# Where a large tile's step turns the next head's q and k: ahead of the second map's scores, or behind them

## The reference

```python
q, k, v = jnp.split(h @ w_in, 3, axis=-1)
q = rms_norm(q.reshape(B, S, H, 2, Dh), q_g)      # H = 8, Dh = 64, two maps per head
k = rms_norm(k.reshape(B, S, H, 2, Dh), k_g)
# per block of 128 queries, chunk-causal mask, scale Dh ** -0.5
s = jnp.where(mask, jnp.einsum('bqhmd,bshmd->bhmqs', qi, k) * scale, -jnp.inf)
p = jax.nn.softmax(s, axis=-1)
pd = p[:, :, 0] - lam * p[:, :, 1]
o = jnp.einsum('bhqs,bshe->bqhe', pd, v)
```

## Time and profile before

| | |
|---|---|
| median of three runs | 2813.56 us (2813.12 to 2814.98) |
| the profiled execution | 2813.21 us, its span 2811.4 us, granted clock 0.992 |
| busy of the span | PE 2725.0 us, PE's weight loads 2373.5, DVE 1898.9, ACT 1501.2, POOL 1077.1 |
| instructions | 42849 |
| longest groups of the attention on PE | projection L417 589.9 and 344.9 us, values L662 279.6 and L664 243.3, scores L559 255.8 and L561 232.5, turned probabilities L634 175.3, turned q and k L509 76.8 |

### The profile page before, as it was taken

One profiled execution on the slowest core, in us unless ns is written; L12 is line 12 of the kernel. 1 busy time (PEld: TensorE's weight loads), 2 busy tenths in 40 slices (PEclk: granted clock), 3 DMA queues, 4 the chain that ended last, 5 costly groups with the idle time before them and its releaser, 6 DMA issues.

```text
span 2811.4 us, 42849 instructions
## 1 busy us (share of the span) xinstructions
PE 2725.0 (97%) x14784; PEld 2373.5 (84%) x14784; DVE 1898.9 (68%) x2726; ACT 1501.2 (53%) x2987; POOL 1077.1 (38%) x956
## 2 busy tenths in 40 slices
PE   7999999999999999979999989999999999999999
PEld 7998989989898999967887778888888888888887
DVE  6777787777778787775776666555555555666655
ACT  5666666666666666654454434444444444344443
POOL 5633334243333424331000444444443444444443
PEclk9999999999999999989999999999999999999999
DMA  8742424243242423224455986666667976666663
GB/s 267 265 138 91 156 96 160 92 145 112 97 150 96 150 96 133 92 90 144 168 173 193 357 330 239 236 236 266 265 242 283 350 286 234 232 235 238 237 237 131
DMA packets 181808, 544.09 MB, mean 194 GB/s; under 512 B 14736, under 2 KB 88208, under 8 KB 136592
## 3 DMA queue, kind: packets, MB, share of 16 engines
q1 hardware_dynamic: 180016, 541.25, 52.8%
q10 hardware_dynamic: 1632, 0.79, 0.1%
HBM read 470.81 MB, written 71.17 MB: 193 GB/s over the span
## 4 chain that ended last, share of the span: by engine, by line
PE 81%; issue 7%; DVE 5%; ACT 3%; DMA 3%; POOL 1%; SPq 1%; ACTq 0%; POOLq 0%; DVEq 0%
PE banks L2159 21%; PE banks L2135 21%; PE banks L417 17%; PE banks L662 5%; PE banks L559 4%; PE banks L561 4%; PE banks L634 3%; PE banks L821 2%; PE banks L664 2%; PE banks L509 2%; DVE mx L578 1%; ACT p_all L601 1%; ACT pt_hi L643 1%; DVE p_all L623 1%; DMA u_factors<-y_stage 1%
## 5 line engine op out<-in xcount | busy, mean ns | idle before, releaser
L2135 PE MATMUL banks<-u,w 128*128 128x512 f32 x2688 | 614.6, 390 | 3.0 <-issue 2.3
L417 PE MATMUL banks<-w_hi,u_ring 128*128 128x384 f32 x2048 | 589.9, 348 | 10.9 <-DVE u_ring L1311 4.3
L2135 PEld LDWEIGHTS banks<-u,w 128*128 128x128 f32 x2688 | 505.4, 188 | 109.2 <-issue 3.3
L2159 PE MATMUL banks<-w,a_hi 128*128 128x512 f32 x1792 | 553.6, 390 | 7.1 <-DVE y L2057 7.1
L1900 POOL TENSOR_TENSOR w<-w_raw,w 128x1024 fp32r<-128x1024 f32 x96 | 246.2, 2578 | 559.5 <-DVE a_lo L2038 281.6
L601 ACT ACTIVATE p_all<-banks,bias 128x1024 f32<-128x1024 f32 (+7 forms) x384 | 331.6, 866 | 182.7 <-DVE bias L581 116.2
L2159 PEld LDWEIGHTS banks<-w,a_hi 128*128 128x128 f32 x1792 | 337.4, 188 | 77.6 <-issue 7.4
L417 PEld LDWEIGHTS banks<-w_hi,u_ring 128*128 128x128 f32 x2048 | 376.4, 189 | 15.6 <-issue 9.7
L2159 PE MATMUL banks<-w,a_lo 128*128 128x512 f32 x896 | 349.4, 390 | 0.0
L447 POOL TENSOR_TENSOR qk_rs<-qk_var,minus_half 128x4 f32<-128x4 f32 x128 | 129.4, 1011 | 564.3 <-DVE qk_var L441 564.3
L417 PE MATMUL banks<-w_lo,u_ring 128*128 128x384 f32 x1024 | 344.9, 337 | 0.0
(11 more groups left out here) (151 smaller groups left out, 4730.5 us busy)
## 6 DMA issues: line engine op xcount, KB each, us to landing
u<-u_factors SPq DMA_DIRECT2D x224, 1024.0 KB, 9.5
u_ring<-u_scratch SPq DMA_DIRECT2D x112, 1024.0 KB, 5.2
w_raw<-in_mlp_w SPq DMA_DIRECT2D x128, 512.0 KB, 6.7
u_scratch<-u_ring SPq DMA_DIRECT2D x16, 1024.0 KB, 5.0
u_factors<-q_hi SPq DMA_DIRECT2D x23, 512.0 KB, 4.4
u_factors<-q_lo SPq DMA_DIRECT2D x23, 512.0 KB, 4.5
w_raw<-in_a_w_in SPq DMA_DIRECT2D x90, 128.0 KB, 4.6
p_all<-in_x SPq DMA_DIRECT2D x16, 512.0 KB, 5.9
```

The lines of the kernel that those rows point to most:

```text
L417: last = pe.matmul(proj[:, 0:3 * HD], u[:, part, kt, :], w[:, kt, :], start=(kt == 0 and part == 0 and w is w_hi), stop=(kt == KT - 1 and ...
L2135: last = pe.matmul(banks[:, UP_BANKS[p] + f, :], w[:, 2 * k2 + k, f * P:(f + 1) * P], u[:, :, part, k, :], start=(STARTS[p] and k2 == 0 an ...
L2159: last = pe.matmul(banks[:, DOWN_BANKS[p] + t, :], a[:, p % 2, f, t * P:(t + 1) * P], b[:, f, :], start=(STARTS[p] and f == 0 and a is a_h ...
```

## The change

In `big_step` of TensorE the four transposes of q and k move from behind the projection's first half to behind the second map's scores, directly ahead of the first turned block of probabilities. In `big_step` of ScalarE the two copies move from behind the first map's exponentials to directly ahead of the copy of that first block. VectorE's and GpSimd's order, `turn_order` with its banks, and all waits stay.

```diff
@@ scalar, big_step
             for k in range(np):
                 act_exp(act, a, 0, k)
-            if n - 1 < ALL:
-                act_turned_qk(act, n - 1)
             if j > BIG:
                 act_square_output(act, a - 2)
             if t >= 1:
                 act_turned_u2(act, t - 1)
             if j == NT - 1 and h + 2 < H:
                 act_split_weights(act, h + 2, (0, 1))
+            if n - 1 < ALL:
+                act_turned_qk(act, n - 1)
             act_turned_p(act, a - 1, 0)
@@ tensor, big_step
             if n < ALL:
                 pe_project(pe, n, 0)
-            if n - 1 < ALL:
-                pe_turn_qk(pe, n - 1)
             if t >= 0:
                 pe_product(pe, t, 0)
                 pe_turn_u2(pe, t - 1)
             pe_scores(pe, a, 1)
+            if n - 1 < ALL:
+                pe_turn_qk(pe, n - 1)
             if t >= 0:
                 pe_product(pe, t, 1, (0,))
             pe_turn_p(pe, a - 1, 0)
```

## The result

| | before | after |
|---|---|---|
| median of 4 runs each | 2814.02 us | 2858.9 us |
| lowest to highest | 2813.12 to 2814.98 | 2857.33 to 2861.84 |
| span of the profiled execution | 2811.4 us | 2855.5 us |
| ratio after / before as recorded | | 1.0152, 95% interval 1.014 to 1.0165 (the two medians alone: 1.0159) |

The account below looks back on a forecast made before the run. TensorE, matmuls filling 97% of the span, was taken to bound the kernel. Later second turned blocks (39.6 us) plus what is late next (2.8) gave 42.4 on 2813.2: 2856 us, own range 2846 to 2866 (0.75), wider range 2837 to 2870.

Parts of the forecast that it names:

- Where: Steps with tiles 8 to 15 in heads 0 to 6, 56 in all, get longer; small steps and MLP as before.
- The scores don't come sooner: Second map's scores: still wait for the first map's exponentials in tiles 8 and 12 to 15; 0.43 us sooner in tile 9.
- The chain X + 2.41: X is the end of the second map's scores; the second L634 can't start before 2.41 us after it.
- The shifts of the second L634: Second block of turned probabilities, tiles 8 to 15: starts 0.49 to 0.93 us later, 5.66 a head, 39.6 in seven.
- What the wait would look like: Idle time on L634 put down to L536 in about 56 steps, 0.4 to 0.5 us each.
- What is late next: Behind L536 in VectorE's queue: the wide maximum and its exponential delay the next scores, 0.4 us a head, 2.8 in all.
- 0.5 us of idle time arises: On TensorE ahead of the second L634 in each changed step: earliest start X + 2.41, against X + 1.91 left alone.
- Rival 4: Worse: all of VectorE's delay reaches TensorE, 8.3 us a head, 58 in all, 2871; chance 0.07.
- Rivals 1 to 3: Wait hidden, 2813, chance 0.04; faster through earlier scores, 2802, 0.04; half, transposes ending sooner and copies hiding 0.1, 2841, 0.10.
- Tile 15's split of weights: ScalarE's L392, now ahead of the copies, ends at 579.6 before they are due at 579.77: no cost.
- The step after tile 15: TensorE idles 2.4 us there, waiting for VectorE and ScalarE; nothing taken back.

Follow-up runs that it names:

- e12: Changed kernel with the first map's first exponential cut to 512 of 1024 columns in large tiles of heads 0 to 6: 2840.93 us, ratio 1.0091.
- e3: Changed kernel with all 12 matmuls of the projection's second half between the two turned blocks, in place of 6: 2858.55 us, ratio 1.0153.
- e5: Changed kernel with the first turned block of probabilities ahead of the transposes of q and k: 2858.42 us, ratio 1.0148.
- e9: Changed kernel with 9 in place of 6 projection matmuls between the two turned blocks: ratio 1.0155.
- e8: Changed kernel with VectorE's second maximum of the second map ahead of q's and k's low parts, and 9 projection matmuls between the turned blocks: ratio 1.0087.
- e4: Changed kernel with 3 matmuls of the projection's second half ahead of the second map's scores, 6 between the turned blocks, 3 behind: 2869.22 us, ratio 1.0191.
- e6: Kernel before, with VectorE making q's and k's low parts ahead of the second map's first maximum in tiles 12 to 15: 2818.98 us, ratio 1.001.
- e1: Kernel before, with the change of ScalarE's order only: 2818.41 us, ratio 1.0012.
- e2: Kernel before, with the change of TensorE's order only: 2864.51 us, ratio 1.0176.
- e11: Kernel before, with the first map's first exponential cut to 512 of 1024 columns in large tiles of heads 0 to 6: 2813.86 us, ratio 0.9992.
- e10: Kernel before, with VectorE's sum of squares of q and k moved from the end of large steps to between the next step's first two maxima: 2834.39 us, ratio 1.0064.

## Why the prediction came out as it did

It said 2856 us, within 2837 to 2870, and slower; 2858.9 was measured. In the spans the loss is 44.1 us where its sum had 42.4. Point by point:

- **Where.** Right: the 56 changed steps alone; small tiles and MLP cost nothing (windows), and the four transposes hold TensorE for 0.43 us in their new place (507.83 to 508.26) as in the old one.
- **The scores don't come sooner** where the transposes had filled a wait for the first exponential (tiles 8 and 12 to 15), and do in tile 9. Right, and shown by e12: with that wait taken away each step of the first kind gets 0.29 to 0.45 back and tile 9 only 0.04. I had 0.43 for five tiles and about half of it for tile 10, 2.37 a head; measured 2.48. That the sums are so near is in part luck: tile 13 has 0.29 where I took 0.43, and tile 11, of which I took nothing, has 0.22.
- **The chain X + 2.41.** Right: 2.42 in tile 8, and link by link (0.63 to ScalarE's copy, 0.79 to VectorE, 0.94 for its two, 0.06 to TensorE). That ScalarE takes the transposes up 0.04 behind their end stood in none of the prediction's rows (in tile 8 before, the copy starts 494.95 - 494.65 = 0.30 behind it, as ScalarE was still at an exponential); the 0.03 measured bears it out. The shifts of the second L634 were to be 0.93, 0.49, 0.71, 0.49 and four times 0.76, 5.66; they were 0.94, 0.51, 0.65, 0.59, 0.82, 0.72, 0.75, 0.82, 5.80 a head. Tile 11 isn't quite like tile 9, since its scores come only 0.27 sooner: 0.10 too little.
- **What the wait would look like.** 56 waits, as said; each shows 0.32, not the 0.4 to 0.5 that I gave. The time is there (first to second L634 in tile 8: 1.99 in place of 1.48) but a part of it is covered by the modelled end of the matmul ahead.
- **What is late next.** In size nearly right, 0.6 a head in place of 0.4. In kind this is the step of the prediction that failed. I treated what stands behind L536 in VectorE's queue as an addition to the bank wait. The runs show a second limit beside it, nearly as long: with the bank wait covered (e3, e5, e9) nothing is gained, and only when the second map's second maximum leaves the queue as well (e8) do 18.3 us come back. So "0.5 us of idle time arises" was a true description and not yet a cause; the cause, in most tiles, is that what must follow the turned q and k, on VectorE as on TensorE, now starts from the end of the second map's scores. In tiles 8 to 11 this is shown by the time that stays behind X, 5.04 and 6.03 us, whether the bank wait is there or not (e3, e9) and whether TensorE has three matmuls less to do there (e4). In tiles 13 to 15 the second limit shows as scores that wait for exponentials and an X that comes later; that these exponentials are late through VectorE's queue is read from e8's gain, by which 0.22 to 0.33 a step come back against e9, and not tested otherwise. In tile 12 the bank is the only limit of the two.
- **Rival 4** (all of VectorE's delay reaches TensorE, 2871) had the mechanism that I left out, but not the price: both limits hang on one point, so their delays don't add. (Its 2871 also lay just above the 2870 up to which I had counted nearly all of it in.) The 2858.9 fits both readings, and the time alone couldn't have told them apart.
- **Rivals 1 to 3.** The wait is not hidden; the scores come sooner (0.41 in tile 9, 0.21 and 0.27 in tiles 10 and 11, at most 0.19 in tiles 13 to 15) and the gain is lost by the chain; the copies hide nothing, the chain is the full 2.42. The waits of the earlier trace rows didn't go, they became one in every step. I had read them as 27 waits of TensorE; they were all on the weight loads' track, where the matmul ahead covers them, and e6, which takes them away, gains nothing. The room seen in the weight loads (84.65 of 94.10 us) took in none of the new waits: the head's large steps grew by 6.2 us while the loads stayed at 83.85. The Trainium skill ("Perfetto Trace Analysis", Identifying the Most-Contended Engine) judges TensorE's headroom by the busy share of the weight loads, together with how much of the peak the matmuls reach. Here that share did not tell whether a wait would lengthen the kernel.
- **Tile 15's split of weights**, at no cost: right, and e1 and e2 show that it needs both halves of the change together (0.6 and 1.1 us a step if one is left out).
- **The step after tile 15**: 0.15 us given back where I took nothing.

Of the loss, then, 17 to 18 us is shown to be the filled wait laid open. The other 27 (e12 over e11) is the chain from X, held in most tiles by two limits at once. What makes up the 24 us by which e8 still lies over the kernel before is open: the filled wait could be 18 of it and k's later low part the rest, but no kernel with e8's edits and the short exponential was run. No version here that computes the whole layer beats the kernel before; e1 and e6, the nearest, lie 0.1% above it.

## What to carry to other kernels

A step that is moved on the engine that bounds the kernel, with nothing added, need not cost anything by itself, and here it did not. Ask which wait it was filling where it stood, and how long the chain from its new place is to the next user of its buffer, against the work that lies between. Then follow the in-order queue of the other engine as far as its next result that the bound engine needs: that may be a second limit as long as the first, and a wait that shows in the trace is then only the one that happens to come first. To find out, relieve both in one kernel, beside each alone; a wait that vanishes without the time moving is the sign of it, or else of a wait that had held up nothing, as in e6. And take such sums apart step by step: here they hid one tile that had only one limit, and three that gave its gain back.

## What the runs showed of the hardware

VectorE and GpSimd took longer for the same instructions where the two ran beside each other for long. In e10 (GpSimd's rows above) the difference of the maps, L623, falls on GpSimd's L453 and L471; VectorE's row of that moment:

```profile
509.96 2.00 DVE L623 SCALAR_TENSOR_TENSOR p_all<-p_all,neg_c 128x1152 f32<-128x1152 f32 x1
```

In the changed kernel's tile 9 the two meet for 0.1 us only, VectorE first, then GpSimd:

```profile
517.51 1.42 DVE L623 SCALAR_TENSOR_TENSOR p_all<-p_all,neg_c 128x1152 f32<-128x1152 f32 x1
```
```profile
517.14 0.47 POOL L471 TENSOR_TENSOR v_s<-rows,v_s 128x128 fp32r<-128x128 f32 x1
```

2.00 against 1.42 us, and 1.58 against 0.47. It isn't a single case: the eight L623 of this form take 1.93 us on average in e10 and 1.42 in the changed kernel. GpSimd's L453, which L623 meets first, kept its 1.04. What the two share was not tested. It is a reason to look at who runs beside an instruction before its duration is taken from another place.
